# One more of 22 feed-forward up-projection pairs in seven block products: 14 in place of 13, two neighbours first, and ScalarE's copies in another order

## What is computed

```python
# first block, for each of 2 layers; x is (1, 512, 1024), D_FF = 2816
h = rmsnorm(x, ffn_norm[l])
u = h @ ffn_w_up[l]                           # (512, 1024) @ (1024, 5632)
a, bv = u[..., :D_FF], u[..., D_FF:]
a = causal_dwconv(a, ffn_conv_w[l], ffn_conv_b[l])   # three taps along the tokens
x = x + (jax.nn.silu(a) * bv) @ ffn_w_down[l]
# ahead of it: three attention-like branches and their projections;
# after both layers: a second block with its own attention branches
```

## Time and profile before

| | |
|---|---|
| median of 3 runs | 1958.09 us |
| the profiled execution's own time | 1960.36 us |
| its span, first to last instruction | 1958.6 us |
| TensorE busy | 1928.6 us, 98% |
| VectorE busy | 1290.1 us, 66% |
| ScalarE busy | 918.2 us, 47% |
| 16 DMA engines, main queue | 30.5% of their time |
| mean granted TensorE clock | 0.997 |
| chain that ended last: TensorE, VectorE | 87%, 8% |

### The profile page before, as it was taken

One profiled execution on the slowest core, in us unless ns is written; L12 is line 12 of the kernel. 1 busy time (PEld: TensorE's weight loads), 2 busy tenths in 40 slices (PEclk: granted clock), 3 DMA queues, 4 the chain that ended last, 5 costly groups with the idle time before them and its releaser, 6 DMA issues.

```text
span 1958.6 us, 31543 instructions
## 1 busy us (share of the span) xinstructions
PE 1928.6 (98%) x11898; PEld 1637.3 (84%) x11898; DVE 1290.1 (66%) x1610; ACT 918.2 (47%) x1401; POOL 30.1 (2%) x60
## 2 busy tenths in 40 slices
PE   7999999999999999999999999999999999999998
PEld 5897889998887897889998888997777777888888
DVE  6866788887645866788887646846664644534435
ACT  5345454555323445455545322344445666544343
POOL 2001000000000001000000000000000000000000
PEclk8999999999999999999999999999999999999999
DMA  7213133333324223133333223533332122232322
GB/s 197 77 46 108 44 107 108 93 102 103 102 76 126 67 56 108 44 103 108 93 107 103 96 82 104 167 86 93 86 112 69 59 82 65 86 119 76 99 89 82
DMA packets 241105, 182.79 MB, mean 93 GB/s; under 512 B 12970, under 2 KB 232360, under 8 KB 240574
## 3 DMA queue, kind: packets, MB, share of 16 engines
q1 hardware_dynamic: 238368, 177.37, 30.5%
q0 software_dynamic: 2160, 2.22, 0.6%
q10 hardware_dynamic: 430, 1.23, 0.2%
HBM read 168.21 MB, written 2.10 MB: 87 GB/s over the span
## 4 chain that ended last, share of the span: by engine, by line
PE 87%; DVE 8%; issue 3%; ACT 2%; DMA 0%; DVEq 0%; ACTq 0%; SPq 0%; POOL 0%
PE ps L882 19%; PE ps L884 18%; PE ps L883 18%; PE ps L1433 4%; PE ps L1432 4%; PE ps L1431 4%; PE ps L669 2%; PE ps L645 2%; PE ps L658 2%; DVE amat L2269 2%; PE ps L1319 1%; PE ps L1318 1%; PE ps L1317 1%; PE ps L521 1%; PE ps L490 1%
## 5 line engine op out<-in xcount | busy, mean ns | idle before, releaser
L882 PE MATMUL ps<-h_hi,w_hi 128*128 128x512 f32 (+1 forms) x1168 | 444.4, 380 | 0.8 <-ACT qk L1636 0.4
L884 PE MATMUL ps<-h_hi,w_lo 128*128 128x512 f32 (+1 forms) x1168 | 434.8, 372 | 0.0
L883 PE MATMUL ps<-h_lo,w_hi 128*128 128x512 f32 (+1 forms) x1168 | 432.7, 371 | 0.0
L2155 DVE TENSOR_TENSOR w_lo<-w_raw,w_hi 128x2048 fp32r<-128x2048 f32 (+3 forms) x110 | 226.9, 2063 | 145.3 <-ACT w_hi L1643 139.6
L1643 ACT ACTIVATE w_hi<-w_raw 128x2048 fp32r<-128x2048 f32 (+3 forms) x108 | 186.9, 1730 | 240.7 <-PE ps L1433 122.0
L882 PEld LDWEIGHTS ps<-h_hi,w_hi 128*128 128x128 f32 x1168 | 219.5, 188 | 43.5 <-issue 6.1
L884 PEld LDWEIGHTS ps<-h_hi,w_lo 128*128 128x128 f32 x1168 | 219.4, 188 | 39.4
L883 PEld LDWEIGHTS ps<-h_lo,w_hi 128*128 128x128 f32 x1168 | 219.6, 188 | 38.9 <-issue 1.9
L2671 DVE TENSOR_TENSOR w_lo<-w_raw,w_hi 128x1024 fp32r<-128x1024 f32 (+1 forms) x118 | 126.5, 1113 | 156.2 <-ACT w_hi L1982 155.4
L882 PE MATMUL ps<-w_hi,h_hi 128*128 128x256 f32 x544 | 152.4, 280 | 0.4 <-DVE h_lo L856 0.4
L883 PE MATMUL ps<-w_lo,h_hi 128*128 128x256 f32 x544 | 150.7, 277 | 0.0
(11 more groups left out here) (437 smaller groups left out, 3738.6 us busy)
## 6 DMA issues: line engine op xcount, KB each, us to landing
w_raw<-in_ffn_w_up_dram SPq DMA_DIRECT2D x88, 512.0 KB, 5.0
w_raw<-in_w_in_dram SPq DMA_DIRECT2D x41, 1024.0 KB, 5.3
w_raw<-in_w_in_dram SPq DMA_DIRECT2D x32, 512.0 KB, 5.1
w_raw<-in_ffn_w_down_dram SPq DMA_DIRECT2D x32, 512.0 KB, 4.3
w_raw<-in_w_out_dram SPq DMA_DIRECT2D x12, 1024.0 KB, 5.1
w_raw<-in_ffn_w_down_dram SPq DMA_DIRECT2D x16, 384.0 KB, 3.7
swapped<-qk SPq DMA_DIRECT2D x96, 64.0 KB, 2.0
w_raw<-in_w_mem_kv_dram SPq DMA_DIRECT2D x4, 1024.0 KB, 5.0
```

The lines of the kernel that those rows point to most:

```text
L882: pe.matmul(dst, lh, rh, start=first and j == 0, stop=False, skip_group_check=read_open)
L883: pe.matmul(dst, lh, rl, start=False, stop=False, skip_group_check=read_open)
L884: ins = pe.matmul(dst, ll, rh, start=False, stop=last and j == len(order) - 1, skip_group_check=read_open)
L2155: dve.tensor_tensor(w_lo[:, slot, 0:n], w_raw[:, slot, 0:n], w_hi[:, slot, 0:n].bitcast(F32), ALU.subtract).then_inc(sem("w_split"), 1)
```

## The change

Pair 4 and the pairs after it are dealt out anew. Plain pairs are now 0, 1, 2, 6, 10, 14, 18, 21; of seven products are 3-4-5, 7-8-9, 11-12-13, 15-16-17, 19-20: 14 in place of 13, in each of the two layers. Four things go with that:

- `HIGH_PLACE` moves `next_up_high(f)` on ScalarE. In the middle pair of a group of three that is not the first group (f = 8, 12, 16) it stands after the first copy; in pair 3 after the second copy; in pair 4 after the third. Elsewhere it stays in front. (For f = 4 the table gives 3, which replaces the 1 of the first rule.)
- `c_sum`, the fourth copy's target, is one buffer in place of two; ScalarE waits until VectorE's `first_gate` of the previous such pair has read it.
- Pairs 19 and 20 are both of seven products now. The rows of `hid` for them lie on `s_raw`, so the copies of pair 19 go to a separate tile `pu_last`, and from pair 19 on ScalarE waits for both parts of `s_lo` before the first copy.
- Since 4 is now in the list, the weight sums of pair 4 are made ahead of VectorE's loop.

```diff
--- before.py
+++ after.py
@@ -59,10 +59,13 @@
 
 LEVELS = (64, 32, 16, 8, 4, 2, 1)
 
-PLAIN_F = (0, 1, 2, 4, 8, 12, 16, 20, 21)
+PLAIN_F = (0, 1, 2, 6, 10, 14, 18, 21)
 FAST_F = tuple(f for f in range(KF) if f not in PLAIN_F)
 FAST_FROM, FAST_TO, FAST = FAST_F[0], FAST_F[-1], len(FAST_F)
 FAST_NO = {f: n for n, f in enumerate(FAST_F)}
+HIGH_PLACE = {f: 1 for f in FAST_F if f - 1 in FAST_NO and f + 1 in FAST_NO}
+if 4 in FAST_NO:
+    HIGH_PLACE.update({3: 2, 4: 3})
 
 
 CREDIT = {"w_split": 2, "tile_done": 1, "x_down": 1, "sq_sum": KD - 1, "raw_lo": KD}
@@ -219,7 +222,8 @@
 
         hid = at("hid", 0, [P, KF, S])
         hid_hi, hid_lo = at("hid_hi", 44, [P, KF, S], F32R), at("hid_lo", 0, [P, KF, S], F32R)
-        y_blk, c_sum = at("y_blk", 33, [P, 768]), at("c_sum", 92.25, [P, 2, 256])
+        y_blk, c_sum, pu_last = at("y_blk", 33, [P, 768]), at("c_sum", 97.25, [P, 256]), at("pu_last", 92.25, [P, S])
+        partial_sums = lambda f: pu_last[:] if f == 19 and 20 in FAST_NO else hid[:, f, :]
         s_raw, s_lo, s_hi = at("s_raw", 38, [P, 3, 4, P]), at("s_lo", 44, [P, 3, 4, P], F32R), at("s_hi", 50, [P, 3, 4, P], F32R)
         t_hi = at("t_hi", 56, [P, 4, 4, 256], F32R)
         t_raw, t_lo = at("t_raw", 72, [P, 4, 4, 256]), at("t_lo", 72, [P, 4, 4, 256], F32R)
@@ -1907,17 +1911,27 @@
                     part = lambda bank, c: ps[:, bank, c * 256:c * 256 + 256]
                     if f in FAST_NO:
                         chain = part(5 + 2 * s, 1)
-                        next_up_high(f)
-                        if f == 19:
-                            act.wait_ge(sem("s_split"), upto(act, "s_split", 2 * FAST_NO[f] + 1))
-                        keep(f, 1, 1, hid[:, f, 256:512], chain)
+                        place = HIGH_PLACE.get(f, 0)
+                        if place == 0:
+                            next_up_high(f)
+                        if f >= 19:
+                            act.wait_ge(sem("s_split"), upto(act, "s_split", 2 * FAST_NO[f] + 2))
+                        keep(f, 1, 1, partial_sums(f)[:, 256:512], chain)
+                        if place == 1:
+                            next_up_high(f)
                         keep(f, 2, 2, part(4 + 2 * s, 0), part(2 * s + 1, 0))
+                        if place == 2:
+                            next_up_high(f)
                         conv_start(f - 1, (f - 1) % 2)
-                        keep(f, 3, 3, hid[:, f, 0:256], chain)
+                        keep(f, 3, 3, partial_sums(f)[:, 0:256], chain)
+                        if place == 3:
+                            next_up_high(f)
                         if f + 1 in FAST_NO:
                             sums_high(f + 1, 0, 2)
                             sums_high(f + 1, 2, 3)
-                        keep(f, 4, 5, c_sum[:, s], chain)
+                        if FAST_NO[f]:
+                            act.wait_ge(sem("fast_sum"), upto(act, "fast_sum", 2 * FAST_NO[f] - 1))
+                        keep(f, 4, 5, c_sum[:], chain)
                         conv_silu(f - 1)
                     else:
                         if f < KF:
@@ -2481,7 +2495,7 @@
 
                     p6 = ps[:, 4 + 2 * (f % 2), 0:256]
                     dve.wait_ge(sem("part_kept"), upto(dve, "part_kept", 4 * FAST_NO[f] + 4))
-                    dve.tensor_tensor(p6, c_sum[:, f % 2], p6, ALU.add).then_inc(sem("fast_sum"), 1)
+                    dve.tensor_tensor(p6, c_sum[:], p6, ALU.add).then_inc(sem("fast_sum"), 1)
 
                 def gate_fast(f):
 
@@ -2497,7 +2511,7 @@
                     s = f % 2
                     dve.wait_ge(sem("part_kept"), upto(dve, "part_kept", 4 * FAST_NO[f] + 3))
                     dve.wait_ge(sem("tile_done"), upto(dve, "tile_done", T_UP + 2 * f + 1))
-                    dve.tensor_tensor(hid[:, f, :], hid[:, f, :], ps[:, 2 * s + 1, :], ALU.add).then_inc(sem("fast_sum"), 1)
+                    dve.tensor_tensor(hid[:, f, :], partial_sums(f), ps[:, 2 * s + 1, :], ALU.add).then_inc(sem("fast_sum"), 1)
 
                 def conv_taps(f, slot):
                     dve.wait_ge(sem("conv0"), upto(dve, "conv0", f + 1))
```

## The result

The changed kernel takes 1968.48 us (median of 5 runs, 1967.71 to 1969.96) against 1958.2 us for the kernel before (5 runs, 1958.04 to 1959.72): the ratio is 1.0048, 95% interval 1.0037 to 1.006. It is slower by 10.3 us, inside the range given (1960.5 to 1971) but outside that of the likeliest case (1963 to 1967.5); the figure forecast was 1965.1.

The account below looks back on a forecast made before the run. TensorE, busy 98%, was taken as the bound. Per layer -2.57 (swap, waits gone) +4.20 +1.14 +0.75 gave +3.52 us, for two layers +7.0 on 1958.09: 1965.1 us; range for 8 in 10, 1960.5 to 1971.

Parts of the forecast that it names:

- the likeliest case: The forecast sum of gains, opening waits and lateness holds: 1963 to 1967.5 us, given 65%.
- What bounds the kernel, and the price of a pair: TensorE, 98% busy, is the limit; a plain pair takes 10.99 us, one of seven products without a wait 9.76 us.
- The value of the swap: One plain pair less and one of seven products more saves 1.23 us per layer.
- The first link, `hidden` of pair 2: Pair 4's p2 waits for `hidden`, starting at 306.09 us after pair 4's early weight sums: +4.20 us per layer.
- The wait in pair 3 ahead of it: At p5 of pair 3 TensorE waits about 1.4 us for the late third copy, at no further cost.
- The second link, chunk 5 copied late: Chunk 5's copy behind pair 4's third copy delays `s_lo`, so pair 5 waits at p2: +1.14 us per layer.
- The lateness in the next group: Chunk 7's high half starts late, which adds to middle pair 8's wait: +0.75 us per layer.
- The bound from above: The 0.75 us lateness comes back in each of four later groups: +2.25 us per layer, 1969.6 us.
- The clock: Rival: stands in pairs 3 and 4 lower TensorE's clock once per layer, 2.7 us each, 1970.5 us; 12%.
- the prediction's own sign: The forecast is wrong in its frame if the clock is below 1.00 anywhere in pairs 3 to 21.
- That the opening is covered: Rival: pair 4's additions fit in VectorE's idle gap, no wait arises, and the time is 1952.9 us; 6%.
- Only pair 4 waits: Rival: pair 5 and the group behind it catch up, +1.63 us per layer, 1961.4 us; 12%.

Follow-up runs that it names:

- e3: The changed kernel regrouped as 3-4, 6-7-8, 10-11-12, 14-15-16, 18-19-20, with pair 5 plain and still 14 pairs of seven products: 1968.49 us.
- e6: The changed kernel with chunk 5's high half behind pair 4's first copy and, in pair 3's turn alone, `hidden` ahead of the weight sums: 1964.48 us.
- e2: The changed kernel with ScalarE's high half of chunk 5 behind the first copy of pair 4 in place of the third: 1964.9 us.
- e1: The changed kernel with 22 extra matmuls of 256 columns in pair 4, ahead of the wait for `hidden` of pair 2: 1966.32 us.
- e7: The changed kernel with chunk 5's high half behind pair 4's first copy and `hidden` ahead of the weight sums in every group's first pair: 1961.06 us.
- e8: Thirteen pairs in the earlier kernel's grouping, `hidden` ahead of the weight sums in groups' first pairs, high half behind the first copy in middle pairs: 1960.45 us.
- e12: The changed kernel with every high half of a chunk back in front of the first copy, in all pairs: 1963.61 us.
- e4: The changed kernel with pair 20 plain, so 13 pairs of seven products, opening with 3-4-5: 1972.07 us.

## Why the prediction was right, and where it was off

**What bounds the kernel, and the price of a pair**: right. The value of the swap, 1.23 us per layer, was met to 0.3 us by the run with pair 20 plain. Pair 20 waits for nobody, as forecast, and pairs 8, 12 and 16 keep their wait. The single `c_sum` and the wait for both parts of `s_lo` cost nothing that shows, as forecast: pairs 19 and 20 take 9.75 and 9.76 us.

**The first link, `hidden` of pair 2**: right to the hundredth, 304.46 us by the sum (306.09 less 1.63) and in the trace. That the weight sums of pair 5 are in that chain is shown by e3, where they are absent and the wait at p2 of pair 4 is gone, and by e6, where they are behind it.

**The wait in pair 3 ahead of it**: there (1.00 us idle, pair 3 of 11.24 us where 11.4 was named), and no further cost.

**The second link, chunk 5 copied late**: right in cause (e2 takes it away, and pair 5 takes 9.75 us) and near in size: pair 5 took 10.93 us in the first layer and 10.72 us in the second, 9.76 + 1.14 = 10.90 us forecast. The step itself came 1.5 us later than the forecast had it, by the clock, and TensorE was as late; the difference stayed.

**The lateness in the next group**: 0.75 us was taken. Pairs 7 and 8 took 10.50 and 10.90 us, against 9.76 and 10.87 of their counterparts 5 and 6 before: 0.77 us. The size is right and the place is not: the forecast added it to the wait at p2 of pair 8, and it came as a wait for the first copy in pair 7, which stands behind the late high half of chunk 8 in ScalarE's queue (338.37 and 340.19 us). That wait has no term in the prediction, so the agreement is in part luck. It did not come back in the later groups. The bound from above counted four of those at 0.75 us and wrote 2.25 us; there are three, and 2.25 us is right.

**The clock** is the term that was mis-sized. It stood as a rival with a chance of 12%, at 2.7 us per layer; it fell in both layers of the change and cost about 1.5 us in each (pairs 3 and 4 together took 25.40 and 25.57 us against 11.4 + 12.5 forecast). So by the prediction's own sign its frame failed: the clock is below 1.00 in the stretch. The range was wide enough to hold the result because it took in that rival's 1970.5 us, not because the sum was near. e1 shows that the stand is the cause and the clock the means: with the stand filled by other matmuls it stays at 1.00, and 2.2 to 2.8 us come back. The sum with it is 3.52 + 1.5 = 5.0 us per layer; measured 5.05 and 4.97. The price had been taken from the start of the program, where the half clock lasted for 13 matmuls of 512 columns; here it was 16 of 256 in the first layer and 15 in the second. And those rows don't show what a stand does to the clock, since it was down before that stand began; the kernel before:

```profile
12.00:14.20 2.20, 1.31 (x8) 0.83 (x8) 2.13 (x4) 0.02 (x1) 2.20 (x5) 1.00 1.00 254
14.30:16.10 1.80, 1.22 (x6) 0.80 (x6) 0.53 (x1) 1.80 (x2) 1.80 (x3) 0.50 1.01 395
```

The Trainium skill, "TensorE: Matmul & The Clock Gate", Part 1, says that activity lifts a throttle that is the default; the trace agrees (0.59 in 306 to 310 us behind the stand, 1.00 again in pair 5), and the weight I gave it was too low.

**Rivals.** That the opening is covered is refuted. "Only pair 4 waits" is refuted for the change and is what happens in e2. The experiments also corrected my own later forecasts: e3, e6, e7 and e8 each left out what ScalarE's queue holds behind one copy.

**Not settled**: why the clock stayed up in one layer and fell in the other behind the same stand of 2.1 us (e6, e7), why it lasted for 14 matmuls in one layer and 27 in the other (e2, e12), and why pairs 4 and 5 of e4 are 0.3 us longer than in the change.

## What to carry to other kernels

When work is added to an in-order engine, write out the chain behind it from the last row that can't have moved, with start-to-start intervals of the same operations from the trace; here that gave the end of the first long wait to a hundredth of a microsecond, and every step behind it 1.5 us too early, because the clock fell there. Do it for each engine whose queue holds a wait, and for every reordering again: moving one long copy (1.9 us) from behind the third kept copy to behind the first decided over some 4 us in one grouping and 8 us in the other, and taking away one wait only laid bare the next queue entry. And price a stand of the matrix engine at more than its length once it is longer than any that the trace shows at full clock.

## What the runs showed of the hardware

- The granted clock fell to 0.5 behind TensorE's stands of 2.6 us (the change, e4), 2.6 and 2.8 us (e2), 2.95 us (e12) and 3.57 us (e3), in both layers each time. In the stretch it stayed at 1.00 behind all stands of 1.0 us and behind those of 1.5 us (e8, both layers). Behind the same stand of 2.1 us (pair 4, e6 and e7) it fell in one layer and not in the other. The stretch then was 1.7 to 1.9 us longer.
- One fall lasted for 14 to 16 matmuls of 256 columns, or for 25 to 27: the latter in the second layers of e2, e3 and e12, with the same program in both layers.
- 22 matmuls whose result nobody reads made the changed kernel 2.2 us faster (2.8 us with each run taken against the kernel before beside it), by keeping that clock up (e1).
- Matmuls of 256 columns start 0.21 us apart at the half clock and 0.113 to 0.12 us at the full one.
